# First block's values from weights and rows in two rounded parts, in four pieces between the keys, the first scores and the convolution

## The reference

```
h = concatenate([meta, x])                        # 272 x 1024
proj = rms_norm(h) @ w_in                         # 1024 -> 6 * 512
q, k, v, cx, cb, cc = split(proj)
attn = diff_attention_group(q, k, v, ...)         # rope on q and k, 4 heads, two softmaxes a head,
                                                  # (p0 - lambda * p1) @ v, rms_norm of each head
conv = cb * centred_depthwise_conv(cc * cx)
h = h + concatenate([attn, conv]) @ w_out
h = h + expert_choice_ffn(rms_norm(h), ...)       # router, 16 experts, 34 rows each, 384 MB of weights
y = rms_norm(h)[16:]                              # to the second block
```

## Time and profile before

| | before |
|---|---|
| median of 3 runs | 1664.34 us (1662.95 to 1664.54) |
| span of the profiled execution | 1661.3 us |
| PE busy | 1491.4 us (90%) |
| DVE busy, ACT busy, POOL busy | 553.6, 419.3, 119.1 us |
| granted TensorE clock, mean | 0.973 |
| DMA | 511.49 MB, 308 GB/s over the span |

### The profile page before, as it was taken

The page is one execution under the profiler, slowest core; times in us unless marked ns, Lnnn a source line. Parts: engine busy times, 40 slices in busy tenths (PEclk is TensorE's granted clock), DMA queues, the critical chain, the costliest instruction groups (busy, mean ns, idle before and its releaser), DMA issues.

```text
span 1661.3 us, 18745 instructions
## 1 busy us (share of the span) xinstructions
PE 1491.4 (90%) x7823; PEld 887.4 (53%) x7823; DVE 553.6 (33%) x968; ACT 419.3 (25%) x868; POOL 119.1 (7%) x121
## 2 busy tenths in 40 slices
PE   9999999988877887888788778899999999999999
PEld 8684433322322322222223223278789899978887
DVE  6573300100100100001001001067776565878843
ACT  5342110000000000000000000066834565446532
POOL 2010000000000000000000000050421110500000
PEclk9999899999998999999999999999999999999999
DMA  9324899999999999999999999956232334555564
GB/s 382 131 102 198 345 405 429 429 434 431 432 430 429 431 431 430 431 430 431 432 431 428 430 429 432 426 194 203 91 114 86 124 115 153 190 166 189 184 198 140
DMA packets 43316, 511.49 MB, mean 308 GB/s; under 512 B 5072, under 2 KB 5328, under 8 KB 27488
## 3 DMA queue, kind: packets, MB, share of 16 engines
q1 hardware_dynamic: 41472, 506.10, 75.0%
q10 hardware_dynamic: 1760, 4.19, 0.8%
HBM read 509.23 MB, written 1.05 MB: 307 GB/s over the span
## 4 chain that ended last, share of the span: by engine, by line
PE 61%; DMA 31%; DVE 5%; ACT 2%; issue 1%; POOL 0%; ACTq 0%; SPq 0%; DVEq 0%; POOLq 0%
DMA sb_ring<-in_w_gate_up 30%; PE PS L715 11%; PE PS L782 9%; PE PS L754 8%; PE PS L1166 6%; PE PS L849 4%; PE PS L816 4%; PE PS L733 2%; PE PS L623 2%; PE PS L922 2%; PE PS L815 2%; PE PS L512 1%; PE PS L520 1%; PE PS L515 1%; PE PS L740 1%
## 5 line engine op out<-in xcount | busy, mean ns | idle before, releaser
L715 PE MATMUL PS<-sb_ring,sb_XG 128*64 128x512 f32 x2048 | 476.5, 620 | 106.7 <-DMA sb_ring<-in_w_gate_up 106.6
L715 PEld LDWEIGHTS PS<-sb_ring,sb_XG 128*64 128x64 f32 x2048 | 151.3, 142 | 426.1 <-issue 272.8
L2108 DVE TENSOR_TENSOR sb_SL<-sb_SL,PS 128x512 f32<-128x512 f32 x32 | 20.6, 683 | 790.3 <-PE PS L715 790.3
L754 PE MATMUL PS<-sb_ring,sb_HT 128*64 128x512 f32 x1024 | 231.3, 608 | 22.9 <-DMA sb_ring<-in_w_down 8.3
L2089 DVE TENSOR_TENSOR sb_wp<-sb_raw,sb_wp 128x1024 fp32r<-128x1024 f32 x157 | 199.5, 1273 | 104.0 <-ACT sb_wp L1362 103.0
L1362 ACT CAST sb_wp<-sb_raw 128x1024 fp32r<-128x1024 f32 x160 | 166.6, 1046 | 107.2 <-PE PS L1166 55.5
L754 PEld LDWEIGHTS PS<-sb_ring,sb_HT 128*64 128x64 f32 x1024 | 84.9, 140 | 159.0 <-issue 127.5
L782 PE MATMUL PS<-sb_hr,sb_wp 128*128 128x256 f32 x1200 | 150.8, 285 | 0.0
L782 PEld LDWEIGHTS PS<-sb_hr,sb_wp 128*128 128x128 f32 x1200 | 145.7, 192 | 3.0 <-issue 2.3
L1374 ACT ACTIVATE sb_SL<-PS 128x512 f32<-128x512 f32 x32 | 17.4, 595 | 514.3 <-PE PS L715 514.3
L816 PE MATMUL PS<-sb_hr,sb_wp 128*128 128x512 f32 x256 | 87.8, 396 | 0.0
(11 more groups left out here) (408 smaller groups left out, 1433.5 us busy)
## 6 DMA issues: line engine op xcount, KB each, us to landing
sb_ring<-in_w_gate_up SPq DMA_DIRECT2D x59, 4096.0 KB, 41.0
sb_ring<-in_w_down SPq DMA_DIRECT2D x29, 4096.0 KB, 40.2
sb_raw<-in_w SPq DMA_DIRECT2D x160, 512.0 KB, 3.3
sb_ring<-in_w_gate_up SPq DMA_DIRECT2D x9, 2048.0 KB, 9.2
sb_ring<-in_w_in SPq DMA_DIRECT2D x12, 1024.0 KB, 16.6
sb_ring<-in_w_down SPq DMA_DIRECT2D x5, 2048.0 KB, 13.6
sb_ring<-in_w_out SPq DMA_DIRECT2D x4, 1024.0 KB, 14.9
sb_ring<-in_w_gate_up SPq DMA_DIRECT2D x2, 1024.0 KB, 9.2
```

The costliest lines, as they stand in the source:

```text
L715: ins = e.matmul(PS[64 * g:64 * g + 64, b, :], m.XG[:, k, r0:r0 + 64], m.ring[s][:, (2 * g + q) * 512:(2 * g + q) * 512 + 512], start=(k = ...
L754: ins = e.matmul(PS[64 * g:64 * g + 64, b, :], m.HT[:, c % 8, (c // 8) * 64:(c // 8) * 64 + 64], m.ring[s][:, a * 1024 + g * 512:a * 1024 ...
```

## The change

The values' weights (slots 4 and 5) become pieces 8 to 11 of the same scheme of two rounded parts, a piece being 1024 consecutive columns of the slot, that is two feature chunks of 512. The convolution's pieces are now 12 to 23. The two 128-row tiles of values are computed by 4 times 12 matmuls 512 wide (high rows by high weights, rest by high, high by rest), with `rotate(7)` after the first piece and the first scores after the second. The meta rows' values stay float32 and move to just behind the fifth key or query (n = 4), with their copy on ACT and their three additions on DVE. The copies of the two tiles come after the first exponentials. The slots 4 and 5 count as used after the second and the fourth piece.

```diff
     def first_piece(self, j):
-        i = j // 2 if j < 8 else 6 + (j - 8) // 2
+        i = j // 2
+        if 8 <= j < 12:
+            c = slice(1024 * (j % 2), 1024 * (j % 2) + 1024)
+            return tuple(v.rearrange("p (k c) -> p k c", k=2) for v in (self.ring[i][:, c], self.wh[j % 5], self.ring_lo[i][:, c]))
...
@@ pe_program @@
+    def meta_values():
+        c0, n = TT[2]
+        b = room(6, "V", 2)
+        for i in range(4, 6):
+            pe.wait_ge(*at("w", i))
+        for k in range(2):
+            for g in range(4):
+                o = (2 * (g % 2) + k) * 512
+                ins = e.matmul(PS[32 * g:32 * g + n, b, :], m.hnT[:, 2 * g + k, c0:c0 + n],
+                               m.ring[4 + g // 2][:, o:o + 512], start=(k == 0), stop=(k == 1), tile_position=(0, 32 * g))
+        ins.then_inc(*mark("pe_proj", "in", "V", 2))
+
+    def value_piece(p):
+        hi, lo = first(8 + p)
+        for ti, (c0, n) in enumerate(TT[:2]):
+            b = room(6 + ti, "V", ti) if p == 0 else 6 + ti
+            for k2 in range(2):
+                k = 2 * p + k2
+                for q, w in ((0, hi), (1, hi), (0, lo)):
+                    ins = e.matmul(PS[:, b, :], m.hnp[q][:, k, c0:c0 + n], w[:, k2, :],
+                                   start=(k == 0 and w is hi and q == 0), stop=(k == 7 and w is lo))
+            if p == 3:
+                ins.then_inc(*mark("pe_proj", "in", "V", ti))
+        if p < 3:
+            ins.then_inc(*mark("pe_proj", "V part", p))
...
         proj(("kq", n), n % 4, n).then_inc(*mark("pe_proj", "in", "kq", n))
+        if n == 4:
+            meta_values()
         if n > 0:
             rotate(n - 1)
-    for ti, (c0, n) in enumerate(TT):
-        b = room((6, 7, 6)[ti], "V", ti)
-        if ti < 2:
-            for k in range(8):
-                pe.wait_ge(*at("w", 4 + k // 4))
-                ins = e.matmul(PS[0:n, b, :], m.hnT[:, k, c0:c0 + n], m.ring[4 + k // 4][:, (k % 4) * 512:(k % 4) * 512 + 512],
-                               start=(k == 0), stop=(k == 7))
...
-        ins.then_inc(*mark("pe_proj", "in", "V", ti))
-        if ti == 0:
-            rotate(7)
...
+    value_piece(0)
+    rotate(7)
+    value_piece(1)
+    scores(0)
+    value_piece(2)
+    value_piece(3)
     for u in range(12):
         if u > 0:
             turn_probs(u - 1)
-        scores(u)
+            scores(u)
         conv(u)
...
@@ act_program @@
         first_hi(n + 4)
+        if n == 4:
+            act.wait_ge(*at("in", "V", 2))
+            e.copy(m.V[0:NM, 2, :], PS[96:96 + NM, banks.of("V", 2), :]).then_inc(*mark("act_proj", "V quarter"))
...
-    for ti, (c0, n) in enumerate(TT):
-        b = banks.of("V", ti)
-        act.wait_ge(*at("in", "V", ti))
...
-    first_hi(12)
+    for j in range(12, 15):
+        first_hi(j)
...
+    exps(0)
+    first_hi(15)
+    first_hi(16)
+    for ti in range(2):
+        act.wait_ge(*at("in", "V", ti))
+        e.copy(m.V[:, ti, :], PS[:, banks.of("V", ti), :]).then_inc(*mark("act_proj", "out", "V", ti))
     for u in range(12):
         if u > 0:
             turned_probs(u - 1)
-        exps(u)
+            exps(u)
...
         if u < 7:
-            first_hi(13 + u)
+            first_hi(17 + u)
...
@@ dve_program @@
         rotated(n)
+        if n == 4:
+            values_sum()
         first_lo(n + 4)
     first_lo(12)
...
+    first_lo(13)
...
-        if 1 <= u < 8:
-            first_lo(12 + u)
+        if u == 0:
+            first_lo(14)
+        elif u < 8:
+            first_lo(16 + u)
...
         softmax(u)
+        if u == 0:
+            first_lo(15)
+            first_lo(16)
         conv(u)
-        if u == 0:
-            values_sum()
...
@@ sp_program @@
         if i < 6:
-            return "in", "V", 2
+            return ("V part", 1) if i == 4 else ("in", "V", 1)
```

More of the change, by code:

```diff
@@ L597, in conv @@
     def conv(i):
-        proj(("conv", i), 5 + i % 2, 8 + i).then_inc(*mark("pe_attn", "in", "conv", i))
+        proj(("conv", i), 5 + i % 2, 12 + i).then_inc(*mark("pe_attn", "in", "conv", i))
+    value_piece(0)
[4 more added lines that the diff above has]
+    value_piece(3)
     for u in range(12):
@@ L1219, in first_hi @@
         w, hi, lo = m.first_piece(j)
-        act.wait_ge(*at("w", j // 2 if j < 8 else 2 + j // 2))
+        act.wait_ge(*at("w", j // 2))
         if j == 4:
@@ L1765, in first_used @@
 def first_used(j):
-    return ("in", "kq", j) if j < 8 else ("in", "conv", j - 8)
+    if j < 8:
+        return "in", "kq", j
+    if j < 11:
+        return "V part", j - 8
+    return ("in", "V", 1) if j == 11 else ("in", "conv", j - 12)
 def piece_done(n):
@@ L1864, in dve_program, with values_sum @@
     e.tensor_reduce(m.l2, lt, AX, ALU.add).then_inc(*mark("dve_norm", "lambda sums"))
+    def values_sum():
+        dve.wait_ge(*at("V quarter"))
+        dve.wait_ge(*at("in", "V", 2))
+        for g in range(3):
+            event = ("out", "V", 2) if g == 2 else ("V sum", g)
+            dve.wait_ge(*now("dve_attn"))
+            e.tensor_tensor(m.V[0:NM, 2, :], m.V[0:NM, 2, :], PS[32 * g:32 * g + NM, banks.of("V", 2), :], ALU.add).then_inc(*mark("dve_attn", *event))
     def rotated(n):
```

## The result

| | before | changed |
|---|---|---|
| median | 1664.09 us (4 runs, 1662.95 to 1664.54) | 1655.46 us (4 runs, 1653.71 to 1656.66) |
| ratio | | 0.9945 (0.9932 to 0.9958) |
| span of the profiled execution | 1661.3 us | 1652.4 us |
| granted clock, mean | 0.973 | 0.978 |
| PE busy | 1491.4 us | 1481.8 us |

By these medians the change makes the kernel 8.6 us faster; the forecast was 1655.7 us. All nine runs of the changed kernel have a median of 1656.51 us, all 44 of the kernel before one of 1663.88, so the gain is better put at some 7.4 us; what makes it vary is told at the end.

What follows compares the result with a forecast made beforehand. PE's steps ahead of the experts' weight stream were taken as the bound, as they release its fetches. Cheaper values 2.84 plus stall 5.81 make 8.65 us, rounded to 8.6: 1664.3 - 8.6 = 1655.7 us, range 1652.0 to 1659.5.

Steps and rivals of the forecast that it cites:

- Pass price: Values of the two tiles: 13.74 us of float32 matmuls become 48 at 0.227 us, 10.90 us; gain 2.84 us.
- rival (c): Values' 48 weight loads of 188 ns no longer hidden, 9.0 us on top, 0.4 us slower: 1664.7 us; chance 0.03.
- Stall: Between meta rows' values and end of first values: 14.87 us holding 9.06 of work; the other 5.81 us all go.
- the clock's part of the stall: Second convolution piece at half clock after PE's idle time, 5.80 us instead of 3.20: 2.60 us to be removed.
- The order laid out in time: PE, ACT and DVE timed from the fifth key or query to first values at 66.1 us; nothing waits.
- The smallest slack: First scores: last rope done at 49.9 us, needed at 51.6, leaving 1.7 us.
- Meta rows at no cost: Their matmuls stay 1.89 us; their additions, moved beside the sixth key or query, are covered, else up to 2.0 us.
- Pass-through of 1: PE time won before the experts' weight stream fills reaches the kernel's end in full, since PE's steps release the fetches.
- Rival (b): Experts' weight stream already runs without pause and swallows the gain: 1664 us; chance 0.04.
- a DMA share of 1.00 before 144 us: Sign of being wrong: DMA engines already fully busy before 144 us, ahead of the experts' stream.
- Rival (a): Clock still falls once in the new order, so only 6.1 us are won: 1658.3 us; chance 0.06.
- The router: Unsteady place, narrow matmuls 5.75 us and filler 8.19 us, where the clock may shift: 3 us allowed either way.

Runs made afterwards that it cites:

- e4: Kernel before, with matmuls nobody reads filling some 2.6 us of PE's 3.2 us idle around the first probabilities and second convolution piece: 1661.09 us.
- e3: Changed kernel with the two tiles' values from float32 rows and weights again, same four pieces and order, their casts and rests left out: 1657.8 us.
- e6: Changed kernel with eight memsets nobody reads on DVE behind the meta rows' three additions, 5.3 us in all: 1657.96 us.
- e2: Kernel before with only the meta rows' values, copy and additions moved behind the fifth key or query; two tiles stay float32: 1661.38 us.
- e5: Changed kernel with twenty float32 matmuls nobody reads on PE after the fourth piece of values, 17.17 us put in: 1674.56 us.
- e1: Changed kernel with the first scores on PE after the fourth piece of values, not between second and third: 1656.99 us.
- e8: Changed kernel with none of the seven filler matmuls on PE while DVE chooses the router's rows: 1656.27 us.
- e9: Changed kernel run again unchanged, seven filler matmuls, in a second session: 1657.69 us against 1664.15 us for the kernel before.
- e10: Changed kernel with three instead of seven filler matmuls at the router, in the second session: 1656.34 us.
- e11: Changed kernel with four instead of seven filler matmuls at the router, run again in the second session: 1654.15 us.
- e7: Changed kernel with four instead of seven filler matmuls on PE while DVE chooses the router's rows: 1654.14 us.

## Why the prediction was right

- *Pass price.* 0.227 us a matmul from the second block, 10.90 us for 48. Measured 2.79 + 2.78 + 5.76 = 11.33 us with the handovers, 0.232 to 0.240 each. The gain is 2.41 and not 2.84 us. The 48 weight loads of 188 ns stayed hidden; rival (c) falls. The Trainium skill ("FP8 and Floating Point Precision", TensorE Precision Notes) gives a true float32 product four passes through the array; as an estimate from that, three passes take 3/4 of 13.74, 10.3 us. The trace shows 1.0 us more.
- *Stall.* 5.81 us forecast, all to go. Removed in full: 14.87 us are now 66.27 - 58.22 = 8.05 us behind the values plus 0.65 for the scores ahead of them, 8.70 of work, a little less than the 9.06 I had summed (the first piece's first eight take 1.00 and not 1.20 us, its turn of probabilities 0.33 and not 0.48). That makes 6.17 us and covers most of what the pass price lacks, which was luck. With the meta rows and the rotation behind them, which took 2.01 and not 1.89 us more (45.78 - 43.77), the sum is 2.41 + 6.17 - 0.12 = 8.46 us at the first values; it was to be 8.65. e4 shows the clock's part of the stall (2.57 us on PE, 2.60 forecast), e3 that the order removes the stall without the new arithmetic.
- *The order laid out in time.* Forecast and measured ends: first piece 48.4 and 48.57, scores 52.2 and 52.46, fourth piece 57.7 and 58.22, first values 66.1 and 66.27. The smallest slack was to be 1.7 us at the scores: the last rope ends at 50.05, the scores start at 51.73. At the first rest I had 2.8 us; by the timeline it is 2.3, and e6 confirms that size.
- *Meta rows at no cost.* 1.84 us amid the keys, nothing waits there. e2 shows the other side: moved alone they win 2.1 us of the time, as the wait for the softmax stays.
- *Pass-through of 1.* 8.48 us at the projection and 0.96 at the router, with 0.5 lost behind it, are 8.9 of span; e5 shows it for 17 us. Rival (b) falls. SP issues the first expert fetch at 58.30 us, forecast for 57.7. One sign of being wrong was ill chosen: a DMA share of 1.00 before 144 us. It stands at 0.95 to 1.03 from 128 to 144 us in the kernel before and at 0.93 to 1.03 from 120 to 136 us in the changed one, and falls to 0.05 and 0.02 behind it; these are single bursts, not the stream.
- *Clock.* Rival (a) falls: 1.00 in every window of 4 us from 40 to 160 us.
- *Range.* The router was given 3 us either way. It moved by 1.0: the narrow matmuls went from 5.75 to 4.09 us, the filler from 8.19 to 8.84, as the clock fell later. What I had not priced is the start and the experts' stream, at the end.
- *Luck.* That 1655.7 met 1655.46 within 0.3 us is luck: the second session's 1657.69 lies 2.0 us off, and the sum held because a smaller gain in the passes met a larger one at the stall and 1.0 us at the router. The 3.0 us from span to median also fitted by chance. In the changed kernel's runs what lies around the span is 1.9 to 2.1 us; the rest, 1.05 us, is that the profiled run (1654.41) lay below its median.

## What to carry to other kernels

A wait that ends last is seldom alone: ask what else PE waits for (here the softmax, done 2.2 us before the additions) before counting the whole stall. An idle stretch of PE has a second price in the matmuls behind it, and one can measure that price alone by filling the stretch with matmuls that nobody reads, as e4 did. A filler, in turn, was worth its time here only until the clock was up and the data were there: three matmuls left the clock low at the gather, seven ended 2.3 us after DVE.

## What was not expected of the hardware

*The first projection runs at either level, by the run.* In e1, e8, e9, e10 and e11 the values start 1.2 us later than in the other traces. In e9 the second and third eight matmuls of the first key take 1.81 and 1.66 us, in the chain of waits:

```profile
15.93 1.30 PE PS L515 x8
17.23 1.81 PE PS L518 x8
19.05 1.66 PE PS L523 x8
```

The window from 12 to 24 us, in e9 and then in the changed kernel's trace, with PE as busy in the one as in the other:

```profile
12.00:24.00 12.00, 10.13 (x62) 9.51 (x60) 11.55 (x25) 7.93 (x13) 0.98 (x1) 0.86 1.01 419
```

```profile
12.00:24.00 12.00, 10.15 (x72) 9.33 (x71) 11.62 (x22) 8.99 (x14) 2.93 (x2) 1.00 1.01 417
```

*The length of a wait does not tell whether the clock falls.* In e2 PE was idle for 2.2 us and the clock fell, for part of what followed; in e4, with the stretch filled but for 0.5 us, it did not. But in e6 PE was idle for 2.7 us, from 45.8 to 48.5 us, and the clock stood at 1.00 all the while and behind it:

```profile
44.00:48.00 4.00, 1.83 (x13) 1.40 (x12) 3.13 (x7) 2.27 (x3) 0.00 (x0) 1.00 0.98 393
48.00:52.00 4.00, 3.50 (x15) 2.91 (x16) 3.76 (x7) 0.43 (x1) 1.72 (x3) 1.00 0.43 178
```

What decides between the two is not shown. The filled stretch kept the clock in e4; an idle one of 2 to 3 us went either way.

*The experts' stage varies, in part by the clock.* From gather to last scatter the traces have 908.10 (e3) to 911.24 us (e9), with the same work; e8's 912.02 and e10's 911.47 hold 2.3 and 1.6 us of low clock at their start. A second part is the clock in the last expert, behind PE's last wait for weights, where no transfer hides it. The same 32 records in e9 and in the changed kernel's trace:

```profile
1057.23 8.81 PE PS L733 x32
```

```profile
1055.59 7.11 PE PS L733 x32
```

These records take 8.60 to 8.81 us in e2, e5, e7, e8, e9 and e10 and 7.11 us in before, changed, e1, e3, e4 and e6; in e1 64 later ones take 15.66 instead of 13.97. That is 1.5 to 1.7 us in seven of the 13 traces. In e11 the clock is low somewhat earlier, where PE would else have waited for weights, and next to nothing is lost. Taken off, together with the low clock at the start, it leaves 908.0 to 909.5 us in all of them. It also tells why e7's gain of 1.80 us at the gather was 0.54 at the second block: 1.6 us went there, and not to the stream.

The second block has 555.0 to 555.7 us in all of them. The 1.2 us of the first projection, the 51.5 to 53.2 us between projection and gather with seven fillers and these 1.7 us are enough to account for runs of one kernel that differ by 4 to 5 us, though each version has one trace only. So a gain of 2 us, such as the filler's, needs more runs than the five here. Why the clock falls in one execution and not in another, and where the last 1.5 us come from, stays open.
